# Expert biases of a mixture-of-experts layer: down biases through the first scatter, up biases by four matmuls of 32 rows

## What is computed

```python
logits = x2d @ w_router + b_router
top_v, top_i = lax.top_k(logits, 4); gates = softmax(top_v)
# for each expert e and each of its tokens
gu = xe @ w_up[e] + b_up[e]                  # 1024 -> 2048
gate = minimum(gu[:, :1024], 7.0)
up = clip(gu[:, 1024:], -7.0, 7.0)
act = (up + 1.0) * gate * sigmoid(1.702 * gate)
y = act @ w_down[e] + b_down[e]              # 1024 -> 1024
out[token] += gate_weight * y
```

## Time and profile before

| | |
|---|---|
| median of three runs | 1434.23 us (1427.08 to 1434.36) |
| span of the profiled execution | 1429.6 us, 16035 instructions |
| PE busy | 1370.5 us (96%) |
| DVE, ACT, POOL busy | 380.7, 222.8, 72.7 us |
| mean granted clock of TensorE | 0.982 of full speed |
| bytes by DMA | 434.16 MB, mean 304 GB/s |
| up weights by PE (L876) | 2048 passes, 444.9 us busy |
| down weights by PE (L896) | 1024 passes, 225.2 us busy |
| biases by PE (L862) | 384 passes, 94.9 us busy |

### The profile page before, as it was taken

The page is one execution under the profiler, slowest core; times in us unless marked ns, Lnnn a source line. Parts: engine busy times, 40 slices in busy tenths (PEclk is TensorE's granted clock), DMA queues, the critical chain, the costliest instruction groups (busy, mean ns, idle before and its releaser), DMA issues.

```text
span 1429.6 us, 16035 instructions
## 1 busy us (share of the span) xinstructions
PE 1370.5 (96%) x6413; PEld 727.7 (51%) x6413; DVE 380.7 (27%) x825; ACT 222.8 (16%) x458; POOL 72.7 (5%) x113
## 2 busy tenths in 40 slices
PE   5999999798999999999999999999999999999997
PEld 3768887576353534435353535353443535353534
DVE  2676753434202031220202020203122020202023
ACT  2143333211010101010101101010101010110101
POOL 5010021223000000000000000000000000000000
PEclk9999998798999999999999999999999999999999
DMA  9332011455889898989989898989898988989880
GB/s 247 119 118 64 1 60 59 170 183 178 359 360 407 358 407 359 410 355 389 358 357 407 355 409 357 407 359 409 357 408 359 389 358 356 404 358 409 358 339 34
DMA packets 74982, 434.16 MB, mean 304 GB/s; under 512 B 8126, under 2 KB 14346, under 8 KB 58572
## 3 DMA queue, kind: packets, MB, share of 16 engines
q1 hardware_dynamic: 73820, 430.11, 75.1%
q0 software_dynamic: 1136, 3.71, 1.0%
HBM read 428.91 MB, written 4.88 MB: 303 GB/s over the span
## 4 chain that ended last, share of the span: by engine, by line
PE 88%; DVE 8%; issue 1%; ACT 1%; POOL 1%; DMA 0%; DVEq 0%; SPq 0%; ACTq 0%; POOLq 0%
PE bank L876 31%; PE bank L896 15%; PE bank L905 14%; PE bank L862 6%; PE bank L856 5%; PE bank L525 3%; PE bank L617 3%; PE bank L807 2%; PE bank L473 2%; PE bank L637 1%; PE bank L674 1%; DVE xb L1359 1%; DVE xb L1355 1%; PE bank L683 1%; PE bank L604 1%
## 5 line engine op out<-in xcount | busy, mean ns | idle before, releaser
L876 PE MATMUL bank<-ring,xb 128*64 128x512 f32 x2048 | 444.9, 592 | 0.0
L876 PEld LDWEIGHTS bank<-ring,xb 128*64 128x64 f32 x2048 | 147.3, 137 | 292.2 <-issue 292.2
L1355 DVE TENSOR_SCALAR xb<-bank 128x512 f32<-128x512 f32 x32 | 22.1, 692 | 844.3 <-PE bank L876 844.3
L896 PE MATMUL bank<-ring,zg 128*64 128x512 f32 x1024 | 225.2, 592 | 0.0
L905 PEld LDWEIGHTS bank<-zg,ob 128*128 128x128 f32 x816 | 196.8, 334 | 13.3 <-issue 13.3
L905 PE MATMUL bank<-zg,ob 128*128 128x128 f32 x816 | 201.4, 404 | 0.0
L896 PEld LDWEIGHTS bank<-ring,zg 128*64 128x64 f32 x1024 | 73.6, 137 | 146.2 <-issue 146.2
L856 PE MATMUL bank<-xb,bT 128*128 128x512 f32 (+1 forms) x204 | 98.4, 611 | 5.8 <-DVE qkv L1374 4.5
L862 PE MATMUL bank<-hT 128*64 128x512 f32 x384 | 94.9, 601 | 0.8 <-ACT xb L1605 0.8
L1610 ACT ACTIVATE zg<-xb 128x512 f32<-128x512 f32 x32 | 20.1, 630 | 460.2 <-DVE xb L1355 460.2
L525 PE MATMUL bank<-hT,ring 128*128 128x288 f32 x320 | 81.0, 414 | 0.0
(11 more groups left out here) (344 smaller groups left out, 892.9 us busy)
## 6 DMA issues: line engine op xcount, KB each, us to landing
ring<-in_w_up SPq DMA_DIRECT2D x128, 2048.0 KB, 12.1
ring<-in_w_down SPq DMA_DIRECT2D x64, 2048.0 KB, 9.5
ring<-in_w_in SPq DMA_DIRECT2D x7, 2048.0 KB, 8.3
ring<-in_w_out SPq DMA_DIRECT2D x2, 2048.0 KB, 7.9
ring<-in_state_gdn SPq DMA_DIRECT2D x4, 512.0 KB, 9.9
out<-ring POOLq DMA_DIRECT2D x1, 2048.0 KB, 12.1
xb<-in_x_prompt SPq DMA_DIRECT2D x1, 1024.0 KB, 5.2
sls<-in_state_gla SPq DMA_DIRECT2D x4, 256.0 KB, 7.1
```

The lines of the kernel that those rows point to most:

```text
L876: last = pe.matmul(bank[g][CAP * h:CAP * (h + 1), :], xeT[:, k, q * CAP:(q + 1) * CAP], w[:, kk, g, h, :], start=False, stop=k == KT - 1, ...
L896: last = pe.matmul(bank[3][CAP * h:CAP * (h + 1), :], aT[:, k, CAP * (u - 4):CAP * (u - 3)], w[:, k, h, :], start=False, stop=u == 5 and k ...
L1355: v.tensor_scalar(gu[:, 0], bank[0][:], 7.0, None, ALU.min).then_inc(sems["gu_ok"], 1)
```

## The change

The down biases leave `down`. Summed over a token's experts, they are the gates (zero for an expert not chosen) times the table `b_down`, and this product is now made by the first scatter. SP loads `b_down` (32 rows of 1024) into the first rows of `yr`; the PE transposes the gates into bank 7 between the halves of the first gather, and ACT copies them into the first 32 rows of `S`. `down` opens its bank with its first weight matmul.

The up biases stay in `up`. The table is laid out by quarters: rows 32 q to 32 q + 31 hold quarter q (512 values) of all 32 experts, loaded by four transfers. One selector of 64 columns, with a one in row e of each group of 32, serves all quarters; each of the four bias matmuls uses 32 rows, group 2 g + h for bank g and half h. Selectors come from `pick`, the sum of the four 32-column blocks of the identity, made once by the DVE. `pick_dn` and POOL's memset of `b_dn` go, and `sel_ok` counts one an expert.

A few semaphores that nobody waits for by another engine are folded into one; that changes no wait.

```diff
-        sel_gu = cut(hTf, 1024, 4, CAP)
-        sel_dn = cut(hTf, 1280, 2, CAP)
+        sel_gu = hTf[:, 1024:1024 + CAP]
+        pick = hTf[:, 1280:1280 + E_N]
...
             load_unit(0, 4)
+            sp.wait_ge(sems["yb_ok"], 1)
+            sp.dma_start(b_dn, a["b_down"][0]).then_inc(sems["ld_bdn"], 16)
             sp.wait_ge(sems["out_done"], 16 * 2)
             load_unit(0, 5)
             sp.wait_ge(sems["p_lg"], 1)
-            sp.dma_start(b_gu, a["b_up"].rearrange("l e (j n) -> (l e j) n", n=512)).then_inc(sems["ld_bias"], 16)
-            sp.dma_start(b_dn[0:2 * E_N], a["b_down"].rearrange("l e (j n) -> (l e j) n", n=512)).then_inc(sems["ld_bias"], 16)
+            for q in range(4):
+                sp.dma_start(b_gu[E_N * q:E_N * (q + 1)], a["b_up"][0, :, 512 * q:512 * (q + 1)]).then_inc(sems["ld_bias"], 16)
...
-            g.wait_ge(sems["p_lg"], 1)
-            c.tick(g.memset(b_dn[2 * E_N:P], 0.0), "bz_ok")
...
-            def start(b, row_of, bias):
-
-                for h in range(2):
-                    pe.matmul(bank[b][CAP * h:CAP * (h + 1), :], row_of[:, h, :], bias, start=True, stop=False, skip_group_check=True)
+            def bias(g, h):
+
+                rows_ = slice(E_N * (2 * g + h), E_N * (2 * g + h + 1))
+                pe.matmul(bank[g][CAP * h:CAP * (h + 1), :], sel_gu[rows_, :], b_gu[rows_, :], start=True, stop=False, skip_group_check=True)
             def up(i, q):
-                pe.wait_ge(sems["sel_ok"], i * 4 + (2 * q + 1))
+                pe.wait_ge(sems["sel_ok"], i * 2 + (q + 1))
                 for g in range(2):
-                    start(g, sel_gu[:, 2 * g:2 * g + 2, :], b_gu)
+                    for h in range(2):
+                        bias(g, h)
...
             def down(i, q):
-                pe.wait_ge(sems["sel_ok"], i * 4 + (2 * q + 3))
-                start(3, sel_dn, b_dn)
...
-                                             start=False, stop=u == 5 and k == 3, skip_group_check=True)
+                                             start=u == 4 and k == 0, stop=u == 5 and k == 3, skip_group_check=True)
...
             gather(0)
+            pe.wait_ge(sems["gate_ok"], 1)
+            for t in range(NTT):
+                last = turn(bank[7][0:E_N, TO[t]:TO[t] + TN[t]], gates[0:TN[t], E_N * t:E_N * (t + 1)], TN[t])
+            last.then_inc(sems["p_gT"], 1)
             gather(1)
-            pe.wait_ge(sems["ld_bias"], 32)
-            pe.wait_ge(sems["bz_ok"], 1)
+            pe.wait_ge(sems["ld_bias"], 64)
+            pe.wait_ge(sems["ld_bdn"], 16)
+            pe.wait_ge(sems["S_ok"], 1)
...
-                v.tensor_copy(sel_gu, bc(ident[:, bass.ds(e * 4, 4)].unsqueeze(2), P, 4, CAP)).then_inc(sems["sel_ok"], 1)
-            def pick_dn(e):
-                v.tensor_copy(sel_dn, bc(ident[:, bass.ds(e * 2, 2)].unsqueeze(2), P, 2, CAP)).then_inc(sems["sel_ok"], 1)
+                v.tensor_copy(sel_gu, bc(pick[:, bass.ds(e, 1)], P, CAP)).then_inc(sems["sel_ok"], 1)
...
                 e = i % PAIRS * 2 + q
-                pick_dn(e)
                 pick_gu(e + 1 if q == 0 else (i + 1) % PAIRS * 2)
...
             v.wait_ge(sems["tri_ok"], 2)
+            c.done(v.tensor_reduce(pick, ident[:].rearrange("p (q e) -> p e q", q=4), AX_X, ALU.add), "v_step")
             pick_gu(0)
...
             rows_in(0, 1)
+            act.wait_ge(sems["S_zero"], 1)
+            act.wait_ge(sems["p_gT"], 1)
+            act.copy(S[0:E_N], bank[7][0:E_N, 0:T]).then_inc(sems["S_ok"], 1)
             rows_in(1, 2)
```

More of the change, by code:

```diff
@@ L106, in program @@
         yr = xb[:, D:2 * D]
+        b_dn = yr[0:E_N]
         gu = cut(xb, 2 * D, 2, 512)
@@ L110, in program @@
         b_gu = hTf[:, 0:512]
-        b_dn = hTf[:, 512:1024]
-        sel_gu = cut(hTf, 1024, 4, CAP)
-        sel_dn = cut(hTf, 1280, 2, CAP)
+        sel_gu = hTf[:, 1024:1024 + CAP]
+        pick = hTf[:, 1280:1280 + E_N]
         zg = sb("zg", [P, KT, T])
@@ L190, in program @@
         names = """ld_x ld_vec ld_gate ld_cst ld_sm ld_bias ld_st ld_router w_in1 w_in2
-            ident_ok masks_ok v_step ss_ok rst_in rst_ok h_ok p_vec vec_ok p_hT
+            ident_ok masks_ok v_step ss_ok rst_in rst_ok h_ok p_vec  p_hT
             hT_ok p_cT cT_ok p_at p_proj proj_ok conv_lin conv_sig conv_ok
-            cs_ok p_convt convt_ok p_gk gk_x gk_e gk_l bT_ok gate_x gate_e
-            gate_l gb_ok p_gt gt_ok gt_exp p_gi di_ok dexp_ok d_ok ss8_ok
+            cs_ok p_convt convt_ok p_gk gk_x gk_e gk_l  gate_x gate_e
+            gate_l gb_ok p_gt gt_ok gt_exp p_gi di_ok dexp_ok  ss8_ok
             rs8_ok qkn_ok p_qkT qkT_ok p_MA MA_ok p_y y_ok p_inv inv_ok
@@ L202, in program @@
             yb_ok sc_ok xe_ok sel_ok S_ok sig_ok ld_w0 ld_w1 ld_w2 ld_w3
-            ld_w4 ld_w5 st_out st_out2 pp_ok bz_ok pad_ok gexp_ok gu_cl ta_ok
+            ld_w4 ld_w5 ld_bdn st_out st_out2 pp_ok S_zero p_gT  gate_ok pad_ok gexp_ok gu_cl ta_ok
             aT_ok ss3_ok rs3_in rs3_ok y_fin""".split()
@@ L431, in _ @@
                 seq_rows(h)
-            g.memset(S, 0.0).then_inc(sems["S_ok"], 1)
+            g.memset(S, 0.0).then_inc(sems["S_zero"], 1)
             g.memset(yr, 0.0).then_inc(sems["yb_ok"], 1)
@@ L969, in _ @@
             v.wait_ge(sems["p_vec"], 1)
-            c.done(v.tensor_copy(vecT[:], bank[7][:, 0:60]), "vec_ok")
+            c.done(v.tensor_copy(vecT[:], bank[7][:, 0:60]), "v_step")
             for k in range(KT):
@@ L1093, in _ @@
                 m = upi[:] if t < 2 else upis[:]
-                c.done(v.tensor_tensor(Dtt[t], Dtt[t], bc(m.unsqueeze(1), n, H, n), ALU.mult), "d_ok")
+                c.done(v.tensor_tensor(Dtt[t], Dtt[t], bc(m.unsqueeze(1), n, H, n), ALU.mult), "v_step")
             for t in range(NTT):
@@ L1117, in _ @@
             for j in range(2):
-                c.done(v.tensor_tensor_scan(bT[:, j, :], resets[:], gE[:, j, :], 0.0, ALU.mult, ALU.add), "bT_ok")
+                c.done(v.tensor_tensor_scan(bT[:, j, :], resets[:], gE[:, j, :], 0.0, ALU.mult, ALU.add), "v_step")
             for t in range(NTT):
@@ L1335, in _ @@
             c.done(v.reciprocal(den[:], den[:]), "v_step")
-            c.done(v.tensor_tensor(e3(gates), e3(gates), c3(den[:].unsqueeze(2)), ALU.mult), "v_step")
+            c.done(v.tensor_tensor(e3(gates), e3(gates), c3(den[:].unsqueeze(2)), ALU.mult), "gate_ok")
             c.done(v.memset(posm[:], 0.0), "v_step")
```

## The result

The changed kernel takes 1384.26 us (median of four runs, 1379.96 to 1388.07), the kernel before 1432.26 us in runs beside it. The ratio is 0.967, with a 95% interval from 0.964 to 0.970: 48.0 us less, where 48.9 were reckoned. (The interval of the ratio allows from 43 to 51 us.) The profiled execution took 1382.88 us with a span of 1381.0.

What follows compares the result with a forecast made beforehand. The prediction took PE in the expert loop as the bound; 27.5 + 18.3 + 3.7 - 0.6 = 48.9 us off the 1434.2 median gave 1385.3, stated as 1386 for small losses, range 1378 to 1416.

Steps and rivals of the forecast that it cites:

- What bounds the kernel: Expert loop: PE is the bound, so a microsecond off its path in a pair is worth 16.
- Down biases: Start of each `down`: removing its two bias matmuls saves 0.86 us a call, 27.5 us over 32 calls.
- Up biases: Bias block of `up`: four tiles at once take 1.14 us in place of 1.72, 18.3 us saved.
- Changes of form: Around the `up` bias block: each change of tile form costs about 0.09 us, the first slot after it 0.05 more.
- Late tiles: Rival, `up` bias block: last tile begins 0.1 to 0.2 us late, 3 to 6 us less saved, about 1391; chance 0.18.
- DVE: End of `swiglu`: one shorter copy brings the first gain 0.23 us earlier a pair, 3.7 us saved.
- One-off work: Before the second gather: PE's small transposes of the gates lose 0.6 us, between 0.4 and 1.2.
- Transfers: Loop's weight loads: a pair needs 398 GB/s at 63.2 us, and units still arrive over 10 us early.
- rival at 1404: Loop: DMA becomes the bound at 390 GB/s, a pair takes 64.5 us, 1.9 saved; chance 0.05.
- One after another: Rival, `up` bias block: every 32-row pass waits for the one before, 33 us lost, 1468; chance 0.05.
- little gained: Rival, between `down` and `up`: the break costs several tenths more, eating the other 30 us, about 1432; chance 0.03.
- two tiles at once: Rival, `up` bias block: row and column halves don't combine, `up` loses 0.28 us, 21.6 saved, 1412.6; chance 0.12.

Runs made afterwards that it cites:

- the last experiment: Changed kernel, but a pair's second up-bias block stands between scatter matmuls and transposes, the other ahead of `down`; selectors copied two at once: 1362.88 us, 0.953 of the kernel before.

## Why the prediction held, point by point

- **What bounds the kernel.** PE, with each microsecond off a pair worth 16. Shown: 3.05 us less a pair (1.72 + 1.14 + 0.23 = 3.09 by the prediction's terms), 48.8 in 16 pairs, 48.0 in the median.
- **Down biases, 27.5 us.** Shown by the kernel with the down part alone: 1.86 us a pair, the 1.72 + 0.14 reckoned for the biases and DVE's copy. The two were not measured apart there.
- **Up biases, 18.3 us.** The doubtful sign came out as taken. In the changed block four first passes begin within 0.02 us, and from its first pass to the first weight pass it is 1.02 us. The kernel with one row group gives the alternative, 1.86. For the up part alone, 1.21 us a pair were measured: 2 x 0.57 = 1.14 for the blocks and 0.10 for the smaller copy, 1.24 together.
- **Changes of form.** 0.09 us for the change and 0.05 for the first slot, from rows of other stages. Measured 0.15 for both together. By the Trainium skill a change of the tiling mode drains the TensorE (TensorEngine Tiling (Array Packing), Key Properties). The trace agrees, with these 0.15 us, which don't turn the sign here.
- **Late tiles.** The rival at 1391 to 1392 is refuted: four tiles begin together. It rested on a misreading. The 0.20 us of the four loads in rows 5 include the length of the last one, about 0.14, so all four start within 0.06 us, and not 0.05 us after each other. By the ratio of the Trainium skill for four row tiles (TensorE: Matmul & The Clock Gate, Measured speedup vs the span model), 3.07, the estimate for the two slots was 1.12 us. From the first pass to the next form they took 1.02, the change included. The block had columns split too, so the case is not quite the one of the Trainium skill.
- **DVE, 3.7 us.** 0.23 us a pair, shown by putting the copies back. Not all of the wait for that gain went: the last experiment took another 0.3 us out of it.
- **One-off work, 0.6 us lost.** From the first gather to the first bias pass it was 352.55 - 340.07 = 12.48 us before and 353.37 - 340.33 = 13.04 after: 0.56. The first gather itself began 0.26 us later; the prediction allowed up to 0.3 for DVE's sum over the identity and took 0, and no run shows whether that sum is the cause. The transposes themselves:

```profile
344.75 1.59 PE L904 MATMUL bank<-zg,ob 128*128 128x128 f32 x6
346.18 0.51 PE L473 MATMUL bank<-ident,ml 128*32 128x128 f32 x3
346.62 5.99 PE L904 MATMUL bank<-zg,ob 128*128 128x128 f32 x24
```

- **Transfers.** Not the bound; 404 GB/s without a wait in the kernel without up biases. The rival at 1404 asked for a pair of 64.5 us.
- **One after another, little gained.** The rivals at 1468 and 1432 fall with the block of 1.02 us and with the up part alone, 1.21 us less a pair. A row of the kernel before already spoke against the first: L784 has the form 32*64 with two column halves, and its 32 passes of 128 columns fit in 1.96 us, where 31 steps of 0.11 us one after another would alone need 3.4.

```profile
327.23 1.96 PE L784 MATMUL bank<-xb,qkv 32*64 32x128 f32 x32
```

- **What was off.** From the end of the last L895 slot to the first weight pass the prediction named 1.2 to 1.3 us as a sign, though its own terms give 0.09 + 0.48 + 0.43 + 0.09 = 1.09; it took 1.12 (762.59 to 763.71). That the whole times came within 0.9 us of the forecast is luck, with an interval of 43 to 51 us; that the pair came within 0.04 is not. The 4.6 us between span and median were taken as fixed; in the execution profiled after, the time stood 1.9 above the span. And with one more run the median of before went from 1434.23 to 1432.26. Both are smaller than the scatter of the runs, in which the 1.7 us between 1386 and 1384.3 lie too. The 12 of 100 kept for two tiles at once stretched the range up to 1416, and nothing came of it. Only a case with four tiles could have closed it, and the rows of the kernel before have none.

## What to carry to other kernels

Where a matmul of few rows and few columns stands on the critical path of the matmul engine, put such matmuls on different row and column groups: eight passes on four tiles took 1.02 us here, on two tiles 1.72 (1.86 with the changes of form). Count the changes of form that this brings (about 0.15 us each here), and put the block where the form changes anyway or, better, where the engine waits for another. And a constant added to every result (a bias under a linear step) can ride on a matmul that runs already: the down biases had cost 27.5 us in the loop, and now cost a few small transposes ahead of it, about 0.6 us.

## What was not expected of the hardware

Four tiles that split both rows and columns start their first passes within 0.02 us of each other, right at the first pass of the form. If the two passes of a matmul stand together in the program, the second passes of the earlier tiles stood ahead of the later tiles' first ones and didn't hold them back; the trace orders passes by time and doesn't show how they stand. And a short vector copy costs less than its drawn length: one drawn 0.19 us long let the next instruction start 0.10 us after it began. The overlap of 0.08 to 0.09 us is the one that the prediction read at the last copy before the gain; on so short a copy it is about half.
